# A gated delta-net's chunk matrices stored at 64 columns instead of 128, in a hybrid attention and expert block

## What is computed

```python
diff = gcum[..., :, None] - gcum[..., None, :]
decay_mat = jnp.exp(jnp.where(causal, diff, -jnp.inf))
a_low = jnp.where(strict, jnp.einsum('bhncd,bhnjd->bhncj', kb, kc) * decay_mat, 0.0)
sol = lax.linalg.triangular_solve(eye + a_low, rhs, left_side=True, lower=True, unit_diagonal=True)
u, w = sol[..., :GDN_V_DIM], sol[..., GDN_V_DIM:]
intra = jnp.einsum('bhncd,bhnjd->bhncj', qc, kc) * decay_mat
def step(state, inp):
    v_new = u_c - jnp.einsum('bhck,bhkv->bhcv', w_c, state)
    o_c = jnp.einsum('bhck,bhkv->bhcv', q_d, state) + jnp.einsum('bhcj,bhjv->bhcv', a_c, v_new)
    state = state * gl[..., None, None] + jnp.einsum('bhck,bhcv->bhkv', k_d, v_new)
```

## Time and profile before

| what | value |
|---|---|
| median of 3 runs | 477.18 us (476.84 to 479.21) |
| the profiled execution's own time | 476.63 us |
| its span | 474.7 us |
| mean granted clock of PE | 0.972 of full |
| PE busy | 441.5 us (93%) |
| DVE busy | 207.7 us (44%) |
| ACT busy | 123.7 us (26%) |
| DMA moved | 137.11 MB, mean 289 GB/s |

### The profile page before, as it was taken

The page is one execution under the profiler, slowest core; times in us unless marked ns, Lnnn a source line. Parts: engine busy times, 40 slices in busy tenths (PEclk is TensorE's granted clock), DMA queues, the critical chain, the costliest instruction groups (busy, mean ns, idle before and its releaser), DMA issues.

```text
span 474.7 us, 10041 instructions
## 1 busy us (share of the span) xinstructions
PE 441.5 (93%) x4213; PEld 331.1 (70%) x4213; DVE 207.7 (44%) x583; ACT 123.7 (26%) x311; POOL 12.5 (3%) x37
## 2 busy tenths in 40 slices
PE   8999999999999999999999899999999787787784
PEld 7885698875988788888645488677685654655451
DVE  1277387996443450711410546343554143412423
ACT  5002523001031230420012634233333122312244
POOL 5010000000000000000000000000000000000001
PEclk9999999999999999999999899999999788988998
DMA  8969957716404050445399879999999999999982
GB/s 310 403 205 347 410 184 252 282 29 204 175 17 162 0 178 1 177 177 178 116 422 420 321 255 423 415 418 422 418 418 418 422 418 420 420 422 420 420 350 104
DMA packets 38176, 137.11 MB, mean 289 GB/s; under 512 B 8560, under 2 KB 9904, under 8 KB 26224
## 3 DMA queue, kind: packets, MB, share of 16 engines
q1 hardware_dynamic: 33776, 135.22, 72.3%
q10 hardware_dynamic: 4352, 1.21, 1.2%
HBM read 134.59 MB, written 1.84 MB: 287 GB/s over the span
## 4 chain that ended last, share of the span: by engine, by line
PE 72%; DMA 19%; DVE 3%; SPq 3%; issue 1%; ACT 1%; POOLq 0%; DVEq 0%; ACTq 0%
PE ps L882 32%; DMA arena<-in_moe_w_up 12%; PE ps L1215 8%; PE ps L1111 6%; PE ps L1096 6%; DMA ring<-in_moe_w_up 6%; PE ps L1258 3%; PE ps L1173 3%; PE ps L1268 3%; PE ps L900 3%; SPq L393 2%; DMA arena<-in_w_in 1%; PE ps L1223 1%; PE ps L999 1%; PE ps L893 1%
## 5 line engine op out<-in xcount | busy, mean ns | idle before, releaser
L882 PE MATMUL ps<-arena 128*128 128x256 f32 (+1 forms) x640 | 156.5, 402 | 0.5 <-DMA arena<-in_w_in 0.5
L882 PEld LDWEIGHTS ps<-arena 128*128 128x128 f32 x640 | 119.8, 190 | 29.7 <-issue 14.9
L1215 PE MATMUL ps<-arena 128*32 128x128 f32 x1072 | 41.9, 301 | 13.3 <-DMA arena<-in_moe_w_up 13.3
L1215 PEld LDWEIGHTS ps<-arena 128*32 128x32 f32 x1072 | 32.4, 117 | 20.6 <-DMA arena<-in_moe_w_up 15.5
L1215 PE MATMUL ps<-ring,arena 128*32 128x128 f32 x912 | 32.8, 285 | 6.8 <-DMA ring<-in_moe_w_up 6.8
L695 ACT ACTIVATE gains<-ps 32x256 f32<-32x256 f32 x62 | 23.4, 378 | 57.3 <-PE ps L1258 56.9
L1215 PEld LDWEIGHTS ps<-ring,arena 128*32 128x32 f32 x912 | 26.0, 111 | 11.9 <-DMA ring<-in_moe_w_up 8.2
L1861 DVE TENSOR_TENSOR masks<-ps,masks 128x64 f32<-128x64 f32 x32 | 7.2, 224 | 58.2 <-ACT masks L676 58.0
L1173 PEld LDWEIGHTS ps<-masks,arena 128*128 128x128 f32 x256 | 30.1, 196 | 2.7 <-issue 2.7
L1173 PE MATMUL ps<-masks,arena 128*128 128x128 f32 x256 | 31.6, 283 | 0.3 <-DVE masks L1798 0.3
L1877 DVE COPY arena<-ps 32x256 f32<-32x256 f32 x62 | 25.8, 416 | 11.4 <-PE ps L1258 10.4
(11 more groups left out here) (273 smaller groups left out, 463.4 us busy)
## 6 DMA issues: line engine op xcount, KB each, us to landing
arena<-in_w_in SPq DMA_DIRECT2D x9, 2048.0 KB, 7.8
arena<-in_moe_w_gate SPq DMA_DIRECT2D x16, 1024.0 KB, 24.2
arena<-in_moe_w_up SPq DMA_DIRECT2D x16, 1024.0 KB, 25.4
arena<-in_moe_w_down SPq DMA_DIRECT2D x16, 1024.0 KB, 24.1
ring<-in_moe_w_down SPq DMA_DIRECT2D x15, 1024.0 KB, 26.4
ring<-in_moe_w_gate SPq DMA_DIRECT2D x14, 1024.0 KB, 23.6
ring<-in_moe_w_up SPq DMA_DIRECT2D x14, 1024.0 KB, 24.9
arena<-in_w_out SPq DMA_DIRECT2D x2, 2048.0 KB, 7.7
```

Source lines behind the costliest of these rows:

```text
L882: last = pe.matmul(out, lhs, rhs, start=(k == 0 and (i > 0 or part % 2 == 0)), stop=(k == KD - 1), skip_group_check=(i == 0))
L1215: last = pe.matmul(c.ps[ROWS * q:ROWS * (q + 1), i % 2, 0:P], c.Hg[:, k, ROWS * i:ROWS * (i + 1)], w[:, :, start:start + 127:2], start=(k ...
```

## The change

The matrices A, T, TT, Yb and attnT get 64 columns per problem: row r of a tile keeps only the 64 columns of its own chunk. `own` holds them as [128, 8, 64]. The first chunk of a tile lies on partitions 0 to 63, the second on 64 to 127. Products with them are issued per chunk (`each_chunk`): lhs and rhs are slices of 64 partitions, and the outputs go to the same 64 partitions of PSUM, so that each uses a quarter of PE's array. Two chunks use the two quarters on the diagonal. wT has 128 output rows, and its two chunks go to two PSUM banks. In `state_out` all products with attnT come first (64x64 weights), then all with qdec. DVE's operations on these matrices have half the columns. The row differences are made by one subtraction per chunk half and one minimum and one maximum, the factor beta is multiplied in by an operation of its own, and the masks of 64 columns are sums of two halves, made once. The store of A takes two DMAs.

```diff
+    c.own = {n: at(n, 512).rearrange("p (a f) -> p a f", a=2 * H) for n in ("A", "T", "TT", "Yb", "attnT")}
...
-    act.wait_ge(s["grow_pre"], 1)
-    act.activation(c.flat["T"], c.flat["T"], ACT.Exp, scale=-1.0).then_inc(s["grow_exp"], 1)
     act.wait_ge(s["grow_pre"], 2)
-    act.activation(c.flat["attnT"], c.flat["attnT"], ACT.Exp).then_inc(s["grow_exp"], 1)
+    act.activation(c.own["T"], c.own["T"], ACT.Exp, scale=-1.0).then_inc(s["grow_exp"], 1)
+    act.wait_ge(s["grow_pre"], 2)
+    act.activation(c.own["attnT"], c.own["attnT"], ACT.Exp).then_inc(s["grow_exp"], 1)
...
-    act.dma_start(tiles_of(c.A_stored), c.flat["A"].rearrange("p (a f) -> p a f", a=2 * H)).then_inc(s["A_stored"], 16)
-    act.wait_ge(s["A_stored"], 16)
+    for m in range(2):
+        act.dma_start(chunks_of(c.A_stored, m), c.own["A"][CHUNK * m:CHUNK * (m + 1)]).then_inc(s["A_stored"], 16)
+    act.wait_ge(s["A_stored"], 32)
...
+    def each_chunk(name, out, lhs, rhs):
+
+        ps = side(name)
+        for i, (t, h) in enumerate(T4):
+            for m in range(2):
+                last = pe.matmul(out(ps, i, m), lhs(t, h, m), rhs(t, h, m), start=True, stop=True)
+        last.then_inc(s["side_ready"], 1)
+
+    def own_out(ps, i, m):
+        return ps[rows(m), CHUNK * i:CHUNK * (i + 1)]
...
-    each("gram", lambda t, h: tile(c.ck, h, t), lambda t, h: tile(c.ck, h, t))
+    each_chunk("gram", own_out, lambda t, h, m: chunk(c.ck, h, t, m), lambda t, h, m: chunk(c.ck, h, t, m))
...
-    each("intra", lambda t, h: tile(c.ck, h, t), lambda t, h: tile(c.cq, h, t))
+    each_chunk("intra", own_out, lambda t, h, m: chunk(c.ck, h, t, m), lambda t, h, m: chunk(c.cq, h, t, m))
...
-        each(f"Y{lv}", lambda t, h: c.A[:, t, h, :], lambda t, h: c.TT[:, t, h, :])
+        each_chunk(f"Y{lv}", own_out, lambda t, h, m: own("A", t, h, m), lambda t, h, m: own("TT", t, h, m))
...
-        each(f"TT{lv}", lambda t, h: c.T[:, t, h, :], lambda t, h: c.Yb[:, t, h, :])
+        each_chunk(f"TT{lv}", own_out, lambda t, h, m: own("T", t, h, m), lambda t, h, m: own("Yb", t, h, m))
...
-    each("u", lambda t, h: c.TT[:, t, h, :], lambda t, h: c.vb[:, t, h, :])
-    each("wT", lambda t, h: c.wrhs[:, t, h, :], lambda t, h: c.TT[:, t, h, :])
+    each_chunk("u", lambda ps, i, m: ps[rows(m), i * P:(i + 1) * P], lambda t, h, m: own("TT", t, h, m), lambda t, h, m: c.vb[rows(m), t, h, :])
+
+    each_chunk("wT", lambda ps, i, m: ps[:, 512 * m + CHUNK * i:512 * m + CHUNK * (i + 1)], lambda t, h, m: c.wrhs[rows(m), t, h, :],
+               lambda t, h, m: own("TT", t, h, m))
...
             for h in range(H):
-                pe.matmul(blk(ps, h), c.attnT[:, t, h, :], c.vn[t][:, h, :], start=True, stop=True)
-                for m in range(2 * t, 2 * t + 2):
-                    own = slice(CHUNK * (m % 2), CHUNK * (m % 2) + CHUNK)
-                    if m:
-                        last_out = pe.matmul(ps[own, h * P:(h + 1) * P], c.qdec[:, t, h, own], c.S[m][:, h, :], start=False, stop=True, skip_group_check=True)
-            last = last_out
+                for m in range(2):
+                    pe.matmul(ps[rows(m), h * P:(h + 1) * P], own("attnT", t, h, m), c.vn[t][rows(m), h, :],
+                              start=(h == 0), stop=False, skip_group_check=True)
+            for h in range(H):
+                for m in range(2):
+                    if 2 * t + m:
+                        last = pe.matmul(ps[rows(m), h * P:(h + 1) * P], c.qdec[:, t, h, rows(m)], c.S[2 * t + m][:, h, :],
+                                         start=False, stop=True, skip_group_check=True)
...
+    chain(v.tensor_tensor(c.own_lower, c.lower[:, 0:CHUNK], c.lower[:, CHUNK:P], ALU.add))
+    chain(v.tensor_tensor(c.masks[:, 8:10, 0:CHUNK], c.masks[:, 8:10, 0:CHUNK], c.masks[:, 8:10, CHUNK:P], ALU.add))
+    settle()
+    chain(v.tensor_tensor(c.own_upper, c.upper[:, 0:CHUNK], c.upper[:, CHUNK:P], ALU.add))
...
+    for m in range(2):
+        own = slice(CHUNK * m, CHUNK * (m + 1))
+        chain(v.tensor_tensor(T[own], ps[own, :, m, :], c.run_sum[own].rearrange("p (a f) -> p a f", f=1).to_broadcast([CHUNK, 2 * H, CHUNK]), ALU.subtract))
+    settle()
+    v.tensor_scalar(attnT, T, 0.0, None, ALU.min).then_inc(s["grow_pre"], 1)
+    v.wait_ge(s["grow_pre"], 1)
+    v.tensor_scalar(T, T, 0.0, None, ALU.max).then_inc(s["grow_pre"], 1)
...
+    chain(v.tensor_tensor(T, T, c.beta_rr.rearrange("p (a f) -> p a f", f=1).to_broadcast([P, 2 * H, CHUNK]), ALU.mult))
...
+    side_done("gram", v.tensor_tensor(c.own["A"], side("gram")[:, 0:512].rearrange("p (a f) -> p a f", a=2 * H), T, ALU.mult))
```

More of the change, by code:

```diff
@@ L901, in each, with rows, chunk, own @@
         last.then_inc(s["side_ready"], 1)
+    def each_chunk(name, out, lhs, rhs):
[4 more added lines that the diff above has]
+        last.then_inc(s["side_ready"], 1)
+    def rows(m):
+        return slice(CHUNK * m, CHUNK * (m + 1))
+    def own_out(ps, i, m):
+        return ps[rows(m), CHUNK * i:CHUNK * (i + 1)]
+    def chunk(ap, h, t, m):
+        return ap[:, h, t * P + CHUNK * m:t * P + CHUNK * (m + 1)]
+    def own(name, t, h, m):
+        return c.own[name][rows(m), H * t + h, :]
     def tile(ap, h, t):
@@ L1029, in state_out @@
     def state_out(n):
-        t, rows = n // 2, slice(CHUNK * (n % 2), CHUNK * (n % 2) + CHUNK)
+        t = n // 2
         ps = side(f"so{n}")
@@ L1035, in state_out @@
             for h in range(H):
-                last = pe.matmul(blk(ps, H + h), c.kdec[rows, t, h, :], c.vn[t][rows, h, :], start=True, stop=True)
+                last = pe.matmul(blk(ps, H + h), c.kdec[rows(n % 2), t, h, :], c.vn[t][rows(n % 2), h, :], start=True, stop=True)
         if n % 2:
             for h in range(H):
-                pe.matmul(blk(ps, h), c.attnT[:, t, h, :], c.vn[t][:, h, :], start=True, stop=True)
-                for m in range(2 * t, 2 * t + 2):
-                    own = slice(CHUNK * (m % 2), CHUNK * (m % 2) + CHUNK)
-                    if m:
-                        last_out = pe.matmul(ps[own, h * P:(h + 1) * P], c.qdec[:, t, h, own], c.S[m][:, h, :], start=False, stop=True, skip_group_check=True)
-            last = last_out
+                for m in range(2):
[6 more added lines that the diff above has]
+                                         start=False, stop=True, skip_group_check=True)
         last.then_inc(s["side_ready"], 1)
@@ L1350, in xT_out, with chunks_of @@
     return c.ps[:, k // 2, (k % 2) * TOK:(k % 2 + 1) * TOK]
-def tiles_of(place):
-    return place.rearrange("(a r) -> a r", a=2 * H)[:, 0:P * P].rearrange("a (p f) -> p a f", p=P)
+def chunks_of(place, m):
+    return place.rearrange("(a m r) -> a m r", a=2 * H, m=2)[:, m, 0:CHUNK * CHUNK].rearrange("a (p f) -> p a f", p=CHUNK)
 def blocks_of(place):
-    return place.rearrange("(q r) -> q r", q=BLOCKS)[:, 0:BLOCK * P].rearrange("q (i f) -> q i f", i=BLOCK)[:, :, 0:BLOCK]
+    return place.rearrange("(q r) -> q r", q=BLOCKS)[:, 0:BLOCK * CHUNK].rearrange("q (i f) -> q i f", i=BLOCK)[:, :, 0:BLOCK]
 def beta_decay_out(c):
@@ L1523, in vector_program, with own8 @@
     chain(v.tensor_tensor(c.beta_rr, c.beta, c.rr[:, 0:8], ALU.mult))
[L1524 to L1530, removed]
+    ps = side("grow").rearrange("p (a m f) -> p a m f", a=2 * H, m=2)
+    T, attnT = c.own["T"], c.own["attnT"]
+    for m in range(2):
[5 more added lines that the diff above has]
+    v.tensor_scalar(T, T, 0.0, None, ALU.max).then_inc(s["grow_pre"], 1)
+    def own8(m):
+        return m.rearrange("p (a f) -> p a f", a=1).to_broadcast([P, 2 * H, CHUNK])
     def masked(buf, mask):
-        return v.tensor_tensor(c.flat[buf].rearrange("p (a f) -> p a f", a=8), c.flat[buf].rearrange("p (a f) -> p a f", a=8),
-                               mask.rearrange("p (a f) -> p a f", a=1).to_broadcast([P, 8, P]), ALU.mult)
+        return v.tensor_tensor(c.own[buf], c.own[buf], own8(mask), ALU.mult)
     v.wait_ge(s["grow_exp"], 1)
     v.wait_ge(s["masks_ready"], 1)
-    chain(masked("T", c.lower))
+    chain(masked("T", c.own_lower))
     settle()
+    chain(v.tensor_tensor(T, T, c.beta_rr.rearrange("p (a f) -> p a f", f=1).to_broadcast([P, 2 * H, CHUNK]), ALU.mult))
     v.wait_ge(s["gsum_exp"], 1)
     chain(v.tensor_tensor(c.bexp, c.beta_rr, c.sums_exp[:, 0:8], ALU.mult))
[L1541 to L1547, removed]
+    settle()
+    side_done("gram", v.tensor_tensor(c.own["A"], side("gram")[:, 0:512].rearrange("p (a f) -> p a f", a=2 * H), T, ALU.mult))
     v.wait_ge(s[f"side_free{side_pair('gram')}"], side_reuse("gram") + 1)
@@ L1551, in vector_program @@
     v.wait_ge(s["grow_exp"], 2)
-    chain(masked("attnT", c.upper))
+    chain(masked("attnT", c.own_upper))
     chain(v.memset(c.inverse, 0.0))
@@ L1556, in vector_program @@
     ps = side("intra")
-    side_done("intra", v.tensor_tensor(c.flat["attnT"], c.flat["attnT"], ps, ALU.mult))
+    side_done("intra", v.tensor_tensor(attnT, attnT, ps[:, 0:512].rearrange("p (a f) -> p a f", a=2 * H), ALU.mult))
     settle()
```

(7 more changed lines are left out.)

15 lines of the change are left out of this document (8 added, 7 removed).

## The result

The changed kernel takes 474.22 us (median of 6 runs, 474.07 to 474.81), the kernel before 478.16 (6 runs, 476.84 to 479.21): ratio 0.992, interval 0.9905 to 0.9935. The forecast of 473.7 us started from a median of 477.18 (3 runs) for the kernel before; the six runs here have 478.16. The profiled execution took 474.81 us, its span is 473.1.

What follows compares the result with a forecast made beforehand. PE was taken to bound the kernel before 212 us. Gains of 2.2 - 0.5 + 1.1 + 0.9 = 3.7 us, less 0.2 for the wait at ma0, took 477.18 to 473.7 us; range 472.3 to 475.8.

Steps and rivals of the forecast that it cites:

- The four narrow groups: gram, intra, Y and TT on PE: each 1.23 us against 1.78, a gain of 0.55, 2.2 for four.
- rival A: The two row tiles take turns wherever they share a PSUM bank: 3.5 us slower, 480.7 us; chance 0.08.
- u and wT: These products on PE: 4.08 us with shape changes against 3.57, a loss of 0.5.
- The outputs: Chunk outputs 1 and 3 on PE, grouped by shape: each 1.02 + 1.02 us, gains of 1.1 and 0.9.
- DVE, ACT, DMA at nothing: DVE's changed operations, ACT's halved exponentials and the changed DMAs: covered by waits, so no gain or loss in time.
- The price of the row differences: On DVE, two subtractions, min and max of 512 columns: 4.3 us at 2.1 ns per column.
- The wait at ma0: PE's start on ma0: the 0.4 us margin after its weights land becomes a wait of 0.15 to 0.2.
- The stall at L1026: PE's one stall in the middle stage, 0.7 us: stays, as its chain of scores, maxima and exponentials is unchanged.
- Rival B: Strips don't come earlier, so the gain ahead of ma0 is lost: 2.45 us gained, 474.7 us; chance 0.1.
- Rival C: Gain real at 212 us but not reaching the end, expert loads holding their pace: 476 to 477 us; chance 0.07.

Runs made afterwards that it cites:

- Experiment 5: Changed kernel with each 64x128 wT product cut into two 64x64 products, using all four quarters of the array: 473.81 us, ratio 0.9917.
- experiment 2: Kernel before with only the chunk outputs grouped by shape, attnT still 128x128 and nothing narrowed: 475.74 us, ratio 0.9962.
- the repeat, experiment 1: The changed kernel run again, unedited, beside the kernel before: 474.17 us, ratio 0.9924.
- experiment 4: Changed kernel with the loops of each_chunk swapped, all products of one chunk half first, then the other: 480.06 us beside 478.68 for the kernel before.
- experiment 7: Changed kernel with four or eight more clears on DVE ahead of the intra product (4.7 and 9.4 us): 474.39 and 483.20 us.

## Why the prediction was right, step by step

The time (473.7 forecast, 474.22 measured), its sign and its mechanism held. Of the 3.45 us at the first load 0.13 are an earlier start and no merit of the forecast; its own terms add up to 3.4, where it had 3.5. By its own steps:

- **The four narrow groups.** Forecast 1.23 with both shape changes, measured 1.08 + 0.19 = 1.27. The step of 0.056, half of 0.111, is 0.058. One thing was wrong in it, and in the section on the change ("each uses a quarter of PE's array"): gram and intra are not 64x64. They contract over all 128 rows, so their passes are 128 rows by 64 columns on two column tiles; only Y, TT and u have 64x64 weights. The two forms cost the same 1.08, so the sum did not notice:

```profile
L914 PE MATMUL ps<-arena x32: 222/222/270, 63.7 to 64.6; 128*64 128x64 f32 x32
```

```profile
116.81 0.57 PE L914 MATMUL ps<-arena 64*64 64x64 f32 x14
```

(the first row is that of L914 alone at gram: ns min/median/max, first and last start, form; the second, the timeline at Y). But rival A, a matter of row tiles, could never have touched gram and intra, so its price of 3.5 us was too high by 2 x (0.34 + 0.55) = 1.8.
- **u and wT.** Forecast 4.08, measured 3.83 + 0.19 = 4.02. Experiment 5 bears out its reason: wT was held by its 128 weight columns.
- **The outputs.** Forecast 1.02 + 1.02, measured the same, twice. But the prediction did not part the grouping from the narrower attnT; experiment 2 shows that the grouping is all of it.
- **DVE, ACT, DMA at nothing.** Right, and for DVE's work ahead of gv's convolution tested, with 4.7 us given back; ACT, DMA and the rest of DVE by the trace alone. The price of the row differences, 4.3 us at the old pace per column, was too high: L1563, L1565 and L1567 take 1.41 + 0.43 + 0.43 = 2.27. The prediction named as cover the 2.11 us ahead of gv's convolution; with what the change freed it was 4.9.
- **The wait at ma0.** Forecast 0.15 to 0.2, measured 0.20, and 0.33 in the repeat. The stall at L1026, now L1054, stayed 0.7.
- **Rival A**, turns by a shared bank: out. Y, TT and u write one PSUM bank from two row tiles, and Y's group takes 1.08, as long as gram's, which has no two row tiles. The Trainium skill, TensorEngine Tiling (Array Packing), "Gotcha 1: PSUM Pressure", says that different row tiles cannot access one bank at the same time; by it Y would take 0.14 + 32 x 0.058 = 2.0, an estimate with the step measured here. For halves that write disjoint partitions of a bank the trace disagrees, and the measurement decides. The order of the products can bring a like effect (experiment 4, 1.83 a group); that its 480.06 us lies near the 480.7 of rival A is chance, as rival A had 2.12 a group and counted the outputs too.
- **Rival B**, the gain ahead of ma0 lost: out, 0.2 was lost of the 1.5 that the three groups ahead gained. **Rival C**: out by experiment 1.

## What to carry to other kernels

List PE's products in order and mark where their weights' rows or columns change between 128 and 64; each change cost 0.14 to 0.19 us here, so products of one shape belong side by side, and that may need no other change (2.07 of 3.45 us). Where a product is cut to half of the array, let neighbours in the order use different tiles, or it gains nothing: the same passes took 1.08 us alternating and 1.83 in turn. And before halving another engine's columns, give it work until the time moves: 4.7 us ahead of gv's convolution did nothing here.

## What the runs showed of the hardware

- **What a step costs.** In the rows of these traces the step of an f32 pass goes by the larger of its weight and its moving columns: 58 ns at 64 and 64 (the records in experiment 4), 0.10 us at 128 and 8 (L944) and 0.111 at 128 and 128, both of the earlier trace rows, 0.111 at 64 and 128 (u, by the sum in experiment 5), and 0.216 at 128 and 256 (L887, 3.46 for 16). It is one step for all tiles that run side by side: two tiles at gram, four at wT's quarters, 14.5 ns a pass, half of the 28 that the earlier trace rows had shown. The Trainium skill, TensorE: Matmul & The Clock Gate, "LDWEIGHTS (loading the stationary operand)", gives the weight load in ns as the columns divided by 1.2: by it, as an estimate, 53 ns for 64 and 107 for 128. The steps of 58 and 111 in the traces lie 4 to 5 ns above.
- **The cost of a shape.** The Trainium skill, TensorEngine Tiling (Array Packing), "Key Properties", says that a change of the tiling mode drains TensorE. What a change costs is read from the rows here: 0.14 into 64 columns, 0.19 into 128 columns by 64 rows, and 0.19 back to the full shape.
- **A short reach.** With the two tiles' products in turn (experiment 4), the second tile started only with 3 of the first one's 16 passes left, and at L999 in the trace of the kernel before with 3 of 8 left. The traces don't say what limits it.
- **A long wait costs twice.** After 5.07 us without work PE was granted 0.50 of its clock (1.2 GHz) and lost another 2.49 us (experiment 7).
